# A two-block transformer kernel: ALPHA kept in the residual, bank sums added by VectorE, layer norm sums ahead of tile 7, centring spread into the next phase

## The reference, cut to what matters

```python
for l in range(DEPTH):
    ada = c_act @ w_ada[l] + b_ada[l]
    sh1, sc1, gt1, sh2, sc2, gt2 = [t[:, None, :] for t in jnp.split(ada, 6, axis=-1)]
    u = x * (1.0 + sc1) + sh1
    y = mixer(u, ...)                 # attention and convolution branches, then @ w_out[l]
    x = layer_norm(DN_ALPHA * x + (1.0 + gt1) * y, ln_mix_g[l], ln_mix_b[l])
    u = x * (1.0 + sc2) + sh2
    h = jnp.square(jax.nn.relu(u @ w_up[l])) @ w_down[l]
    x = layer_norm(DN_ALPHA * x + (1.0 + gt2) * h, ln_ffn_g[l], ln_ffn_b[l])
```

## Time and profile before

| what | value |
|---|---|
| median of 3 runs | 1778.9 us |
| the profiled execution | 1778.8 us |
| its span, first to last instruction | 1777.1 us |
| TensorE busy | 1735.2 us, 98% |
| VectorE busy | 1367.4 us, 77% |
| ScalarE busy | 934.1 us, 53% |
| GpSimd busy | 292.6 us, 16% |
| mean granted TensorE clock | 0.994 of full speed |
| moved from memory | 345.65 MB read |

### The profile page before, as it was taken

The page is one execution under the profiler, slowest core; times in us unless marked ns, Lnnn a source line. Parts: engine busy times, 40 slices in busy tenths (PEclk is TensorE's granted clock), DMA queues, the critical chain, the costliest instruction groups (busy, mean ns, idle before and its releaser), DMA issues.

```text
span 1777.1 us, 26832 instructions
## 1 busy us (share of the span) xinstructions
PE 1735.2 (98%) x11282; PEld 1560.4 (88%) x11282; DVE 1367.4 (77%) x1830; ACT 934.1 (53%) x1173; POOL 292.6 (16%) x219
## 2 busy tenths in 40 slices
PE   6999999999999999999999999999999999999998
PEld 5888898888888888889888898898888998998887
DVE  5998654798789988687988779878755699778754
ACT  6554454655355544466554445756544546556433
POOL 1000000230210001050000149510001099010000
PEclk9999999999999999999999999999999999999999
DMA  7667543467676767524676643354554443435552
GB/s 267 238 260 269 182 156 110 163 260 262 239 273 258 260 242 267 195 96 174 252 261 247 227 167 143 122 187 143 189 189 177 157 163 122 143 134 190 189 190 80
DMA packets 53240, 348.42 MB, mean 196 GB/s; under 512 B 6769, under 2 KB 10114, under 8 KB 13058
## 3 DMA queue, kind: packets, MB, share of 16 engines
q1 hardware_dynamic: 53122, 346.73, 53.6%
HBM read 345.65 MB, written 1.05 MB: 195 GB/s over the span
## 4 chain that ended last, share of the span: by engine, by line
PE 85%; DVE 9%; ACT 3%; DMA 2%; POOL 1%; issue 0%; SPq 0%; ACTq 0%; DVEq 0%; POOLq 0%
PE bank L904 38%; PE bank L903 20%; PE bank L860 7%; PE bank L862 6%; PE bank L861 6%; DVE wl L1941 3%; DMA raw<-in_chunks 2%; ACT wh L1474 1%; DVE bank L2413 1%; PE bank L875 1%; DVE arena L2432 1%; DVE xx L1963 1%; PE bank L1409 1%; PE bank L885 1%; DVE arena L2431 0%; DVE arena L2460 0%
## 5 line engine op out<-in xcount | busy, mean ns | idle before, releaser
L1941 DVE TENSOR_TENSOR wl<-raw,wh 128x2048 fp32r<-128x2048 f32 (+1 forms) x279 | 641.1, 2299 | 250.4 <-ACT wh L1474 250.0
L904 PE MATMUL bank<-xx,wh 128*128 128x512 f32 x1920 | 669.4, 393 | 0.0
L1474 ACT ACTIVATE wh<-raw 128x2048 fp32r<-128x2048 f32 (+1 forms) x279 | 525.9, 1885 | 192.3 <-DMA raw<-in_chunks 192.1
L903 PE MATMUL bank<-xx,wl 128*128 128x256 f32 x1920 | 539.3, 281 | 14.9 <-DVE wl L1941 14.6
L904 PEld LDWEIGHTS bank<-xx,wh 128*128 128x128 f32 x1920 | 360.2, 188 | 80.6
L904 PE MATMUL bank<-hx,wh 128*128 128x512 f32 x1216 | 422.0, 390 | 0.0
L903 PEld LDWEIGHTS bank<-xx,wl 128*128 128x128 f32 x1920 | 363.2, 189 | 16.0 <-issue 15.0
L903 PE MATMUL bank<-hx,wl 128*128 128x256 f32 x1216 | 343.4, 282 | 1.1 <-DVE wl L1941 1.1
L860 PE MATMUL bank<-xx,wh 128*128 128x256 f32 x1008 | 293.2, 291 | 2.5 <-ACT arena L1608 1.4
L861 PE MATMUL bank<-xx,wh 128*128 128x256 f32 x1008 | 286.6, 284 | 0.0
L862 PE MATMUL bank<-xx,wl 128*128 128x256 f32 x1008 | 286.6, 284 | 0.0
(11 more groups left out here) (332 smaller groups left out, 1951.1 us busy)
## 6 DMA issues: line engine op xcount, KB each, us to landing
raw<-in_chunks SPq DMA_DIRECT2D x263, 1024.0 KB, 4.8
arena<-in_ada SPq DMA_DIRECT2D x48, 1024.0 KB, 6.9
raw<-in_chunks SPq DMA_DIRECT2D x16, 768.0 KB, 4.2
arena<-in_bias_rows SPq DMA_DIRECT2D x1, 2048.0 KB, 12.8
x<-in_x SPq DMA_DIRECT2D x4, 256.0 KB, 4.2
arena<-in_w_uk SPq DMA_DIRECT2D x1, 1024.0 KB, 4.8
arena<-in_w_uv SPq DMA_DIRECT2D x1, 1024.0 KB, 9.0
out<-x SPq DMA_DIRECT2D x8, 128.0 KB, 2.1
```

Of the source, the lines that this page charges most:

```text
L903: pe.matmul(o[:, 0:T], lo_w, halves[:, 0, :], start=start, stop=False, skip_group_check=True)
L904: return pe.matmul(o.rearrange("p (h t) -> p h t", h=2), hi_w, halves, start=False, stop=stop, skip_group_check=True)
L1474: act.activation(wh[:, c % RING, at], raw[:, c % RING, at], ACT.Copy).then_inc(hi_made.sem, 1)
L1941: dve.tensor_tensor(wl[:, c % RING, at], raw[:, c % RING, at], wh[:, c % RING, at].bitcast(F32), ALU.subtract).then_inc(lo_made.sem, 1)
```

## The change

1. x is kept multiplied by ALPHA in front of both adds. A small tensor vecA holds ALPHA times the gains and biases (final norm and layer norms), made by one VectorE step at the start; gain and bias steps read it (`residual`), except in the last layer norm. The adds then need no factor on x.
2. VectorE adds the result straight from the bank, scaled by (1 + gate), to x. ScalarE's scaling and the buffer are gone. In the mixer these are two steps of one tile instead of one step of two tiles.
3. In the mixer, tile 6 is summed in bank 0 and has a signal of its own (tile_done). The early sum stands after the first 4 of 8 inner steps of tile 6 instead of after tile 6. VectorE splits the chunk after the third one behind its early part instead of ahead of it.
4. In `pe_ln` all sums that don't need tile 7 stand ahead of it; squares of 6 and 7 are apart; the late columns lie in bank 4 and have a signal.
5. The padding is 4, 4 and 6 matmuls instead of 6, 6 and 7.
6. Centring: tiles 0, 1 before the variance, 2, 3 after it, 4, 5 and 6, 7 behind the first and the second scaling of the next phase (in ln1b behind the reciprocal).

```diff
 pe_out
                     if KIND[s] == "mix":
-                        pe.wait_ge(y_out.sem, y_out.at(s, j - 1))
+                        pe.wait_ge(x_ready.sem, x_ready.at(s, 2 * (j - 1)))
...
                 for m in range(2):
-                    if KIND[s] == "mix" and j == 3 and m == 1:
-                        pe_early(NEXT[s])
                     for k in range(KT):
-                        last = three(bank[2 + j % 2][:, m * T:(m + 1) * T], ...
+                        if KIND[s] == "mix" and (j, m, k) == (3, 0, 4):
+                            pe_early(NEXT[s])
+                        last = three(out_bank(s, j, m), ...
                                      start=(k == 0), stop=(k == KT - 1))
+                    if KIND[s] == "mix" and (j, m) == (3, 0):
+                        last.then_inc(tile_done.sem, 1)
 pe_ln (new part)
+            keep_clock(4)
+            pe.wait_ge(x_ready.sem, xr(s, 6))
+            pe.matmul(LATE, ones[:, :], x[:, 6, :], start=True, stop=False)
+            columns(LATE_COLS, x, 6, True, False)
+            pe.wait_ge(six_folded.sem, six_folded.at(s))
+            columns(SQUARE_COLS, sixq, 0, True, False)
+            if s[3] == "a":
                 pe.wait_ge(sq_made.sem, sq_made.at(s, 3))
                 for k in (4, 5):
                     columns(SQUARE_COLS, xn, k, False, False)
             pe.wait_ge(sq_made.sem, sq_made.at(s, 4))
+            columns(SQUARE_COLS, xn, 6, False, False)
+            pe.wait_ge(x_ready.sem, xr(s, 7))
+            pe.matmul(LATE, ones[:, :], x[:, 7, :], start=False, stop=True).then_inc(late_sum.sem, 1)
+            columns(LATE_COLS, x, 7, False, True).then_inc(late_cols.sem, 1)
+            pe.wait_ge(sq_made.sem, sq_made.at(s, 5))
+            columns(SQUARE_COLS, xn, 7, False, True).then_inc(stat_made.sem, 1)
+            keep_clock(4)
 dve_mod
             for k in range(KT):
+                if KIND[before] == "ln":
+                    dve.wait_ge(cen_made.sem, cen_made.at(before, 3 + k // 2 + 1))
                 dve.scalar_tensor_tensor(out=xn[:, k, :], in0=x[:, k, :], scalar=fold[:, i, 0, k:k + 1], in1=src,
...
                     rest(k - 1)
+                if KIND[before] == "ln" and k in (0, 1):
+                    dve_centred(before, 2 + k)
 dve_ffn
-                            dve.wait_ge(y_out.sem, y_out.at(s, k + 1))
...
-                            dve.scalar_tensor_tensor(out=x[:, k, :], in0=x[:, k, :], scalar=ALPHA, in1=qy[:, k % 4, :],
+                            dve.scalar_tensor_tensor(out=x[:, k, :], in0=bank[2 * (g % 2) + m][:, 0:T], scalar=ada(int(s[2:]), 5, k, 1), in1=x[:, k, :],
                                                      op0=ALU.mult, op1=ALU.add).then_inc(left_added.sem, 1)
 dve_mix
             for j in range(4):
-                dve.wait_ge(y_out.sem, y_out.at(s, j + 1))
-                xs = flat(x[:, 2 * j:2 * j + 2, :])
-                dve.scalar_tensor_tensor(out=xs, in0=xs, scalar=ALPHA, in1=yt[:, j % 2, :], op0=ALU.mult, op1=ALU.add).then_inc(x_ready.sem, 1)
                 if j < 3:
+                    dve.wait_ge(chunk_used.sem, c0 + 22 + j + 1)
+                for m in range(2):
+                    if j == 3:
+                        dve.wait_ge(*((tile_done.sem, tile_done.at(s)) if m == 0 else (chunk_used.sem, c0 + 26)))
+                    k = 2 * j + m
+                    dve.scalar_tensor_tensor(out=x[:, k, :], in0=out_bank(s, j, m), scalar=ada(l, 2, k, 1), in1=x[:, k, :],
+                                             op0=ALU.mult, op1=ALU.add).then_inc(x_ready.sem, 1)
+                if j < 2:
                     lo(c0 + 22 + j + AHEAD)
                 if j == 2:
                     dve_early(NEXT[s])
                     dve.wait_ge(late_moved.sem, late_moved.at(NEXT[s]))
+                    lo(c0 + 22 + j + AHEAD)
 dve_ln
+            dve_centred(s, 0)
             dve.wait_ge(stat_made.sem, stat_made.at(s))
             dve.wait_ge(dsq_made.sem, dsq_made.at(s))
...
+            dve_centred(s, 1)
             dve.wait_ge(root_made.sem, root_made.at(s))
             dve.reciprocal(col[:, 2, :], col[:, 1, :]).then_inc(inv_made.sem, 1)
-            centred(3).then_inc(cen_made.sem, 1)
             if s == STAGES[-1][1]:
+                dve_centred(s, 2)
+                dve_centred(s, 3)
                 dve_ln_gain(s)
```

More of the change, by code:

```diff
@@ L507, in vec, with out_bank, residual @@
         return vecT[:, tile, row:row + 1]
+    def out_bank(s, j, m):
+        return bank[0 if KIND[s] == "mix" and (j, m) == (3, 0) else 2 + j % 2][:, m * T:(m + 1) * T]
+    def residual(s, row):
+        return vec(0, row) if s == STAGES[-1][1] else vecA[:, row - V_FINAL:row - V_FINAL + 1]
     G_PE = {n: i + 1 for i, n in enumerate(["z", "G", "kt", "A", "kv", "o", "ostat", "ospread"])}
@@ L1411, in columns @@
                 return last
-            def first_six(start):
-                pe.wait_ge(six_folded.sem, six_folded.at(s))
-                return columns(SQUARE_COLS, sixq, 0, start, False)
-            folded_first = s[3] == "b"
-            if folded_first:
-                first_six(True)
-            keep_clock(6)
-            for k in (6, 7):
-                pe.wait_ge(x_ready.sem, xr(s, k))
-                last = pe.matmul(LATE, ones[:, :], x[:, k, :], start=(k == 6), stop=(k == 7))
-            last.then_inc(late_sum.sem, 1)
-            for k in (6, 7):
-                columns(LATE_COLS, x, k, k == 6 and not folded_first, k == 7)
-            if not folded_first:
+            keep_clock(4)
[5 more added lines that the diff above has]
+            if s[3] == "a":
                 pe.wait_ge(sq_made.sem, sq_made.at(s, 3))
@@ L1430, in pe_ln @@
                     columns(SQUARE_COLS, xn, k, False, False)
-                first_six(False)
             pe.wait_ge(sq_made.sem, sq_made.at(s, 4))
-            for k in (6, 7):
-                last = columns(SQUARE_COLS, xn, k, False, k == 7)
-            last.then_inc(stat_made.sem, 1)
-            keep_clock(6)
+            columns(SQUARE_COLS, xn, 6, False, False)
[5 more added lines that the diff above has]
+            keep_clock(4)
             pe.wait_ge(inv_made.sem, inv_made.at(s))
@@ L1575, in act_ffn @@
             for g, j, c, _, _ in down_chunks(s):
-                if KIND[s] == "sq" and j == len(DOWN["sq"]) - 1:
-                    for m in range(2):
-                        act.wait_ge(*((tile_done.sem, tile_done.at(s, g + 1)) if m == 0 else (chunk_used.sem, c + 1)))
-                        k = 2 * g + m
-                        if k >= 4:
-                            act.wait_ge(left_added.sem, left_added.at(s, k - 3))
-                        act.activation(qy[:, k % 4, :], bank[2 * (g % 2) + m][:, 0:T], ACT.Identity,
-                                       scale=ada(int(s[2:]), 5, k, 1)).then_inc(y_out.sem, 1)
                 if g >= 1 and j == 0 and KIND[NEXT[s]] == "rms":
@@ L1874, in act_mix, with act_mix_out @@
             hi(c0 + 21 + AHEAD)
[L1875 to L1889 removed]
+            act_mix_out(s, c0 + 22)
+        def act_mix_out(s, c0):
+            for j in range(3):
+                hi(c0 + j + AHEAD)
                 if j == 2:
                     act_early_mean(NEXT[s])
[L1892 to L1894 removed]
+                    for q in range(3):
+                        act_square(NEXT[s], q)
         def act_early_mean(s):
@@ L2001, in dve_early @@
             late = x[:, 6:8, :]
-            dve.scalar_tensor_tensor(out=late, in0=both, scalar=-1.0 / ALPHA, in1=late, op0=ALU.mult, op1=ALU.add).then_inc(late_moved.sem, 1)
+            dve.scalar_tensor_tensor(out=late, in0=both, scalar=-1.0, in1=late, op0=ALU.mult, op1=ALU.add).then_inc(late_moved.sem, 1)
             for q in range(3):
@@ L2352, in dve_mod @@
                 dve.wait_ge(spread.sem, spread.at(before))
-                dve.wait_ge(cen_made.sem, cen_made.at(before))
             else:
```

68 lines of the change are left out of this document (28 added, 40 removed).

## The result

The changed kernel takes 1788.34 us (median of 6 runs, 1786.87 to 1789.14) against 1778.84 us for the kernel before (6 runs, 1774.99 to 1782.79). The ratio of the two is put at 1.004, 95% interval 1.0025 to 1.0055. So it is slower, by 7 us by the ratio and by 9.5 us by the medians, where 1780.3 us had been predicted and 1784.6 was the end of the range. The profiled execution took 1788.77 us with a span of 1787.0 us.

The account below looks back on a forecast made before the run. TensorE is busy 98%, so only the four layer norms count: +0.85 (ln0a) + 0.15 (ln0b) + 0.65 (ln1a) - 0.3 (ln1b) = +1.35 us. 1778.9 + 1.4 = 1780.3 us, range 1776.4 to 1784.6.

Parts of the forecast that it names:

- The small step at the start: Kernel start: multiplying 75 columns of scalars by ALPHA is hidden by TensorE's wait of 14.6 us.
- The eviction path: Mixers and feed-forwards: dropped ScalarE scalings and changed VectorE steps are hidden beside the big matmuls; counted at nothing.
- The forecast's clock: Layer norms after mixers: granted clock stays at 2.4 GHz in the first block's, falls to 0.50 in the second's, as before.
- falls at one more layer norm: Rival: clock falls at one more layer norm, or earlier in it; 3 us more, 1783.3 us; chance 0.33.
- its own mark, 0.50 in ln0a: Sign deciding for the extra clock fall: the profile shows 0.50 in the first block's layer norm after the mixer.
- Hold-up of the fold: Layer norms after mixers: GpSimd's fold waits behind VectorE's weight split, over 2 us instead of 1.33; TensorE waits 0.7 us.
- without the hold-up of the fold it is 0.7 us sooner: Bound for the sums after a mixer; as a rival with half-hidden centrings, 1777.6 us, chance 0.10.
- Nothing is won: Layer norm after a mixer: adds of tiles 6 and 7 end at about 1196.1 and 1196.6; before, both by 1196.5.
- First chunk: Next phase after three layer norms: two centrings between the scalings delay the last tile, +0.85 us each, bounds 0 to 1.2.
- ln0b and ln1b: Layer norms after feed-forwards: the first starts spreading 0.7 us sooner, net +0.15 us; the second, ending the kernel, -0.3 us.
- ln1a: Second block's layer norm after the mixer, clock at 0.50: TensorE follows VectorE less closely, so +0.65 us.

Follow-up runs that it names:

- e1: Kernel before with an unused 75-column tensor where the change puts vecA, displacing the arena by 320 bytes; 1785.19 us, ratio 1.0025.
- e2: Changed kernel with vecA allocated behind the arena, so hx and all else lie where they lay before; 1782.72 us, ratio 1.0012.
- e3: e2 with the split of the weight chunk ahead of the early mean's steps again, as in the kernel before; 1778.63 us, ratio 0.9996.
- e4: e2 with the padding of the kernel before, 6, 6 and 7 matmuls instead of 4, 4 and 6; 1785.94 us, ratio 1.0026.
- e5: e3 with the centring of tiles 4, 5 and tiles 6, 7 put back behind the reciprocal; 1777.38 us, ratio 0.9975.
- e6: e3 with the four first pads moved from in front of the layer norm's sums to inside them; 1777.84 us, ratio 0.9974.
- e7: e3 without the four first pads at all four layer norms; 1775.69 us, ratio 0.9960.
- e10: e5 and e7 together; 1774.40 us, ratio 0.9953 to the kernel before.
- e15: Changed kernel with only the weight chunk's split put back ahead of the early mean's steps, arena still displaced; 1783.55 us, ratio 1.0012.
- e11: Kernel before without its six first pads at each layer norm, nothing else; 1784.04 us, ratio 1.0018.

## Why the prediction was wrong

**The step that failed** is "The small step at the start (75 columns of scalars times ALPHA) is hidden by the wait of 14.6": the sum has no other term for vecA. No run shows a cost of its time. But its result needs room, the room displaced the arena by 320 bytes, and each of 1,216 pairs of matmuls of the down products became 3.4 ns longer: +4.1 us by that product, +4.5 by e1. Without it the measured 1788.3 would have been about 1784, inside the range. The prediction went through the instructions that the change adds and never through the arrays. A view of before can't price this, but the list of arrays shows that it happens; an unused array of the same size is the test. The eviction path itself, which the prediction counted at nothing, held: from the end of the first block's last down product to ln0a, e2 and e3 lose at most 0.1 us against the kernel before, and in the down products of sq0 and sq1 nothing.

**The forecast's clock.** I took it as likelier that the clock stays up in ln0a than that it falls at one more layer norm. The rival came true by its own mark, 0.50 in ln0a. It was priced at 3 us. In the profile of after, ln0a is 4.0 us longer where the sum had 0.85; with the arena at its old place 2.5 us longer (low for 6.8 us, not 10.2). So its price is 1.6 to 3.2 us in these profiles. But the mark tells less than I thought: the premise that the kernel before keeps its clock in ln0a stood on one profile, and five of six profiles of its instructions with displaced arrays have 0.50 there, at 15.5 to 17.6 us from big matmul to lower half instead of 14.66. What the change adds on average is the difference in mean clock, 0.0026 for the changed kernel and 0.0015 for e2. Over the 93 timed executions of the kernel before 0.001 of clock goes with 0.9 us, so this is an estimate of 2.3 and 1.3 us. Forecast plus this rival plus the placement, 1780.3 + 3 + 4.1 = 1787.4, is the measured time to 1 us; that it comes so close is in part luck, as the ledger below has other entries.

**Hold-up of the fold: right, its counterfactual too small.** The order (split, adds, fold at over 2 us, TensorE idle ahead of the fold's columns) came as written; the fold's columns were put at 1197.8, 3.2 us behind the big matmuls' end at 1194.6, and came 3.0 behind it. The bound "without the hold-up of the fold it is 0.7 us sooner" was too little: in e3 they come 1.3 us sooner, because tile 6 is then in time as well. The prediction saw the split move and wrote "Nothing is won"; it did not say that the split's new place, and not the hoisted sums, was what lost. The Trainium skill's rule on the port that VectorE and GpSimd share (SBUF — State Buffer, "SBUF: two separate sides") agrees with the runs as to who waits: 3.19 us in the changed kernel, e2 and e4, 1.28 to 1.29 us in e3, e5, e6, e7, e10 and e15. Behind the split's end 1.1 us of the fold were left, a little less than the 1.29 that it takes when free.

**First chunk: right.** +0.85 us was taken; from the scaling to the last lower half it is 7.37 us against 6.51, in ln0a, ln0b and ln1a alike, and e5 takes it away again.

**ln0b and ln1b: right.** ln0b 13.23 to 13.38 is the +0.15 of the sum, with the scaling 0.70 us sooner (the prediction had 0.7 for the spreading ahead of it). From the end of sq1 to the end of the kernel it is 0.2 us less (0.3 predicted).

**ln1a: within what the clock's place makes of it.** +1.08 us against +0.65, with a low stretch of 6.8 us in both. The same instructions took only +0.07 in e2, whose low stretch is as long and begins 1.1 us later behind the last big matmul. So neither number confirms the 0.65.

**What the ranges left out.** The sum of the schedule's terms was +1.35. The profiled pair gives 4.0 + 0.15 + 1.1 - 0.2 = 5.1 us for the same places, of which about 3.2 are the clock in ln0a. The other 4.8 us of the 9.9 are the down products (4.0), the stage "even" (2.0, of which the low stretch at 301 us is some 1.4) and the start (0.5), less 1.0 us in the second layer's mixer, where the low stretch is 3.4 us in the changed kernel and 6.8 in the profile of before, and less small things. None of the stretches at 301 us and in the mixer is shown to come or go with the change.

## What to carry to other kernels

Read what a change does to the arrays, not only to the instructions: allocate new small arrays behind the large ones, and when a ledger of matched matmuls shows a loss that grows evenly through code that was not touched, run the old kernel with unused room of the same size. When work is hoisted on one engine, look at what it pushed back in the queue of the engine that feeds it: here one step of 2.3 us that came to stand ahead of the adds decided more than the hoisting. Padding that keeps the clock is free only where TensorE would idle: if a later edit fills that wait, take the padding out and measure again. And one profile is one draw of the clock's low stretches: before a stretch that stays up is taken for a property of the kernel, compare the mean clock over several executions.

## What the runs showed of the hardware

- The pace of a long row of matmuls depends on where its right operand lies within 128 bytes relative to other arrays: 0.3467, 0.3489, 0.3501 and 0.3511 us a pair for 0, 32, 64 and 96 bytes of displacement. The delays of single pairs follow short patterns (at 96 bytes 0.356, 0.353, 0.344, repeated).
- An up product of one kernel runs at 0.3467 or at 0.3533 us a pair, and which of them differs from phase to phase and from execution to execution: e3 and e5 have the same instructions up to ln0a, and the second up product is at 0.3467 in one and 0.3533 in the other. At six up products and some 2 us each this would be, with the clock's low stretches, enough for the 13 us by which executions of the kernel before differ. Only the profiles show the paces; the timed runs have no trace. They have their mean clock, and over the 93 of the kernel before it accounts for about a fifth of the variance of the time (correlation -0.46), so most of the spread is not explained by it.
- In the profiles that have a low stretch in ln0a, it begins 4 to 7 us after the last big matmul, and its place and length differ between kernels whose instructions up to there are the same: from none to 6.8 us among the kernel before and the six that add only unused room to it.
- The mean granted clock over some twelve executions tells such kernels apart better than one profile: 0.9897 without the six first pads of the kernel before (e11), 0.9933 with them, 0.9950 with four pads inside the sums (e6).
